# Two transformer blocks on one core: linear attention 12 and dilated attention 4 plan steps sooner, stick order turned, dilated values in 512 columns

## What is computed

```python
nx   = rmsnorm(x, attn_norm_g)
gq, gk, gv, gr, glow, dq, dk, dv = split(nx @ w_in)
o_a  = gla_mixer(gq, gk, gv, log_sigmoid(glow @ gate_w2 + gate_b) / 16)   # linear attention, 4 heads
o_a  = per_head_norm(o_a) * gla_norm_g * silu(gr)                          # gr is "gG" below
o_b  = dilated_mixer(dq, dk, dv, rel_bias)                                 # 8 heads, three patterns
h    = x + concat(o_a, o_b) @ w_out
h    = h + square(relu(rmsnorm(h) @ w_ff1)) @ w_ff2
x2   = rmsnorm(h, final_norm_g)
# second layer
q, k, v, q_hg, f_hg, i_hg, g_hg, gates = split(rmsnorm(x2) @ w_in_2)
o_sb = stick_breaking_attention(norm(q), norm(k), v)   # A = sigmoid(z) * product of (1 - sigmoid)
o_hg = hgrn2_mixer(q_hg, f_hg, i_hg, g_hg)
h    = x2 + (sigmoid(gates) * branch outputs) @ w_out_2
out  = h + (silu(hn @ w_gate) * (hn @ w_up)) @ w_down
```

## Time and profile before

| what | us |
|---|---|
| median of 3 runs | 1362.75 |
| lowest and highest of them | 1362.65, 1363.94 |
| the profiled execution, its own time | 1364.07 |
| span of the profiled execution | 1362.7 |
| PE busy in the span | 1348.6 (99%) |
| DVE busy | 873.2 (64%) |
| ACT busy | 819.9 (60%) |
| granted TensorE clock | 1.00 |

### The profile page before, as it was taken

The page is one execution under the profiler, slowest core; times in us unless marked ns, Lnnn a source line. Parts: engine busy times, 40 slices in busy tenths (PEclk is TensorE's granted clock), DMA queues, the critical chain, the costliest instruction groups (busy, mean ns, idle before and its releaser), DMA issues.

```text
span 1362.7 us, 19539 instructions
## 1 busy us (share of the span) xinstructions
PE 1348.6 (99%) x7510; PEld 1135.7 (83%) x7510; DVE 873.2 (64%) x1548; ACT 819.9 (60%) x1235; POOL 334.6 (25%) x306
## 2 busy tenths in 40 slices
PE   9999999999999999999999999999999999999999
PEld 6977956789899898887777788888888898889889
DVE  6055466577576682357787779975437785568557
ACT  6575566753544545666577767775666645754553
POOL 0211101235343251111211121211113252315214
DMA  7976643925436137876654685668888536824733
GB/s 251 238 165 144 148 117 78 231 32 196 99 98 179 33 125 191 193 169 144 149 129 111 137 217 125 137 145 182 201 214 203 110 118 194 184 47 164 188 51 109
DMA packets 57969, 202.45 MB, mean 149 GB/s; under 512 B 6450, under 2 KB 7019, under 8 KB 57748
## 3 DMA queue, kind: packets, MB, share of 16 engines
q0 software_dynamic: 25632, 93.09, 36.4%
q1 hardware_dynamic: 31380, 106.24, 23.7%
q10 hardware_dynamic: 864, 1.87, 0.4%
HBM read 199.05 MB, written 2.12 MB: 148 GB/s over the span
## 4 chain that ended last, share of the span: by engine, by line
PE 77%; DVE 11%; ACT 8%; DMA 3%; issue 2%; SPq 0%; POOL 0%; DVEq 0%; ACTq 0%
PE bank L660 18%; PE bank L667 18%; PE bank L664 18%; PE bank L698 17%; DVE eb L1730 2%; PE bank L813 1%; ACT WL L1038 1%; ACT eb L1198 1%; ACT WH L1030 1%; ACT zs L1152 1%; PE bank L885 1%; DVE eb L1725 1%; DMA WL<-in_w_in 1%; DMA WL<-in_w_gu 1%; DMA RAW<-in_w_in 1%
## 5 line engine op out<-in xcount | busy, mean ns | idle before, releaser
L660 PE MATMUL bank<-NH,WH 128*128 128x512 f32 x1152 | 459.8, 400 | 0.3 <-ACT NH L1207 0.3
L664 PE MATMUL bank<-NL,WH 128*128 128x512 f32 x1152 | 448.1, 390 | 0.6 <-DVE NL L1470 0.5
L667 PE MATMUL bank<-NH,WL 128*128 128x512 f32 x1152 | 448.1, 390 | 0.6 <-DVE WL L1465 0.4
L660 PEld LDWEIGHTS bank<-NH,WH 128*128 128x128 f32 x1152 | 216.5, 188 | 60.2 <-issue 17.8
L667 PEld LDWEIGHTS bank<-NH,WL 128*128 128x128 f32 x1152 | 216.2, 188 | 47.5 <-DVE WL L1465 0.8
L664 PEld LDWEIGHTS bank<-NL,WH 128*128 128x128 f32 x1152 | 216.8, 188 | 44.7 <-DVE NL L1470 1.6
L1030 ACT ACTIVATE WH<-RAW 128x1024 fp32r<-128x1024 f32 (+3 forms) x148 | 152.1, 1032 | 74.4 <-PE bank L667 39.0
L698 PE MATMUL bank<-AH,WH 128*128 128x256 f32 x644 | 182.5, 283 | 0.3 <-DVE AL L2115 0.3
L698 PE MATMUL bank<-AL,WH 128*128 128x256 f32 x644 | 182.2, 283 | 0.0
L698 PE MATMUL bank<-AH,WL 128*128 128x256 f32 x644 | 182.2, 283 | 0.0
L1038 ACT ACTIVATE WL<-WH 128x1024 fp32r<-128x1024 f32 (+1 forms) x146 | 153.3, 1052 | 12.2 <-DMA WH<-in_w_in 9.9
(11 more groups left out here) (375 smaller groups left out, 2115.3 us busy)
## 6 DMA issues: line engine op xcount, KB each, us to landing
WL<-in_w_in POOLq DMA_DIRECT2D x58, 512.0 KB, 7.2
RAW<-in_w_gu SPq DMA_DIRECT2D x44, 512.0 KB, 5.1
WL<-in_w_gu POOLq DMA_DIRECT2D x34, 512.0 KB, 8.0
RAW<-in_w_ff SPq DMA_DIRECT2D x32, 512.0 KB, 4.6
WH<-in_w_in POOLq DMA_DIRECT2D x32, 512.0 KB, 7.1
RAW<-in_w_in SPq DMA_DIRECT2D x28, 512.0 KB, 6.4
quarters<-in_w_ff SPq DMA_DIRECT2D x24, 512.0 KB, 4.7
WL<-in_w_ff POOLq DMA_DIRECT2D x17, 512.0 KB, 6.5
```

The source lines that it names most:

```text
L660: e.matmul(o, a[0], a[1], start=(k == 0), stop=False)
L664: e.matmul(o, b[0], b[1], start=False, stop=False)
L667: mm = e.matmul(o, c[0], c[1], start=False, stop=(k == t.kt - 1))
```

## The change

- `T_D`, the origin of the linear attention, is 12 plan steps ahead of the start of `qD`. `T_A1`, that of the dilated attention, is 4 ahead of the start of `wo0` (now called `W0`), and its period is 2.4.
- `vD` is one weight unit of 512 columns with four token tiles. Tiles 0 and 1 are interleaved block by block, then 2 and 3: two blocks of the one, two of the other, four blocks in turn, two of the one, two of the other. The copy on ACT takes 512 columns.
- In stick-breaking DVE does scan and difference for p = 0 and then for p = 1, and likewise masked copy and minimum.
- DVE's last multiplication of the `hq`, `hf` and `hg` gates moves from 9.0 (`hg`: 11.0) to 11.3, and ACT's logarithm of `hf` from 9.2 to 11.5, on the scale of `calm`.
- The `gG` sigmoids use two rows of `mixed` as scratch in place of two of the linear attention's buffers, so DVE's differences there no longer wait for gates.

```diff
-        add("vD", "w_in", 9, 11, 8, UC)
+        units.append(("vD", "w_vd", None, 8, 512, 0))
...
-                elif st == "vS" and c:
+                elif st == "vS" and c or st == "vD" and c % 2:
...
+            if st == "vD":
+                for first, second in (mine[0:2], mine[2:4]):
+                    second.v0, first.v1 = first.v0, second.v1 - 2
...
-            many = len(tiles) > 2
+            many = len(tiles) > 2 or tiles[0].st == "vD"
...
-        T_D = plan.start("qD")
-        T_A1, R1 = plan.start("wo0"), 3 * 0.71
+        T_D, W0 = plan.start("qD") - 12.0, plan.start("wo0")
+        T_A1, R1 = W0 - 4.0, 2.4
...
-            return plan.used[p - HL] + (1.3 if plan.used[p - HL] == T_A1 else 0.1)
+            return plan.used[p - HL] + (1.3 if plan.used[p - HL] == W0 else 0.1)
...
-                    yield max(t.v1 + (1.4 if t.v1 == T_A1 else 1), ready_columns[ph])
+                    yield max(t.v1 + (1.4 if t.v1 == W0 else 1), ready_columns[ph])
...
-                    n = min(t.cols, S if st == "vS" else UC)
+                    n = min(t.cols, S if st in ("vD", "vS") else UC)
...
-                    yield calm(t, 9.2)
+                    yield calm(t, 11.5)
                     act.wait_ge(("hf_f", t.i))
...
-            streams += silu_gates("gG", lambda i: mixed[:, i, :], gt_, lambda i: [("gate", "gG", i - 2)] if i >= 2 else [])
+            streams += silu_gates("gG", lambda i: mixed[:, i, :], [mixed[:, 4, :], mixed[:, 5, :]],
+                                  lambda i: [("gate", "gG", i - 2)] if i >= 2 else [("band", i)])
             streams += [gla(0), gla(1)]
-            streams += [mixed_split("mixed", k, T_A1 - 2.0 + 0.2 * k, [("gla_out", k), ("product", "block", plan.last_unit("vD"), k)])
+            streams += [mixed_split("mixed", k, W0 - 2.0 + 0.2 * k, [("gla_out", k), ("product", "block", plan.last_unit("vD"), k)])
...
-                    yield calm(t, 11.0 if st == "hg" else 9.0)
+                    yield calm(t, 9.0 if st == "gG" else 11.3)
...
-                decay(64, B64, d0, [("gla_out", 1)] if c else [("gate", "gG", 2)])
+                decay(64, B64, d0, [("gla_out", 1)] if c else [])
...
-                decay(128, B128, d1, [] if c else [("gate", "gG", 3)])
+                decay(128, B128, d1, [])
...
                             scan.then_inc(*dve.sig("stick_sum", s - 1, p))
-                        for p in range(2):
                             dve.wait_ge(("stick_sum", s - 1, p))
                             e.tensor_tensor(z[p], z[p], ee[p], ALU.subtract).then_inc(*dve.sig("stick_log", s - 1, p))
...
                             low_.then_inc(*dve.sig("stick_b", s, p))
-                        for p in range(2):
                             dve.wait_ge(("stick_b", s, p))
...
-                    yield calm(t, 9.0)
+                    yield calm(t, 11.3)
                     dve.wait_ge(("sigmoid", ("hf", t.i)), ("lb", 6))
...
+    a["w_vd"] = cut(np.ascontiguousarray(w_in[:, 2576:3088]), 8, 512)[0]
```

More of the change, by code:

```diff
@@ L2143, in vector @@
             streams += [put("qG", qG, 0.125), put("kG", kG)]
-            streams += silu_gate("gG", lambda i: mixed[:, i, :], lambda i: g_gla[:, i:i + 1], gt_, [])
+            streams += silu_gate("gG", lambda i: mixed[:, i, :], lambda i: g_gla[:, i:i + 1],
+                                 [mixed[:, 4, :], mixed[:, 5, :]], [])
             streams += [gla(0), gla(1), put("qD", qD, 0.125), put("kD", kD)]
-            streams += [mixed_split("mixed", k, T_A1 - 2.0 + 0.2 * k, []) for k in range(4)]
+            streams += [mixed_split("mixed", k, W0 - 2.0 + 0.2 * k, []) for k in range(4)]
             streams += [dilated(), to_h("wo0", "wo0", lambda k: x_in(k)[-1])]
@@ L2407, in lay_out @@
     x_t = x["x"][0].T.reshape(8, P, S).transpose(1, 0, 2).reshape(P, 8 * S)
-    a["w_in"] = cut(np.concatenate([w_in[:, 0:512], w_in[:, 768:1536], w_in[:, 1552:3088]], 1), 8, UC)
+    a["w_in"] = cut(np.concatenate([w_in[:, 0:512], w_in[:, 768:1536], w_in[:, 1552:2576]], 1), 8, UC)
+    a["w_vd"] = cut(np.ascontiguousarray(w_in[:, 2576:3088]), 8, 512)[0]
     a["w_vg"] = cut(np.concatenate([w_in[:, 512:768], w_in[:, 1536:1552]], 1), 8, UC + 16)[0]
```

## The result

The changed kernel takes 1370.22 us (median of 10 runs, 1367.45 to 1375.0) where the kernel before takes 1363.87 in the same series: a ratio of 1.0047, with an interval of 1.0037 to 1.0058, so 6.4 us slower. The prediction was 1365.0 with a range of 1356.8 to 1368.0. The direction was right, and the time lies outside the range. The profiled execution took 1370.22 us with a span of 1368.9, 6.2 more than before.

A forecast was written before the change was run, and what follows sets the result against it. PE, at full granted clock with few waits, was taken to bound the kernel. Terms -1.3 + 2.4 + 2.7 + 0.9 + 2.8 - 1.9 - 3.2 = +2.4 us on 1362.75 gave 1365.0 us, range 1356.8 to 1368.0.

The forecast's parts named there:

- the chain of the linear attention: Linear attention, c = 0: PE waits ahead of the diagonal products for work queued behind gate tile 2; +2.4 us.
- the level behind it: Linear attention, c = 0, products after the diagonal ones: lost lead and newly interposed DVE and ACT work; +2.7 us.
- c = 1: Linear attention, second pass: a weight piece and `kD`'s second copy slip ahead of its chain; +0.9 us.
- the dilated start: Dilated attention 4 steps sooner: waits at scores 1, first transposes and first value products, 4.0 for 1.2 us; +2.8 us.
- the dilated values: `vD` matmuls: 96 of 512 columns in place of 192 of 256; -1.3 us.
- its granted clock is full throughout: PE, whole kernel: the clock stays full, so edits are worth only PE work or waits removed; no clock cost counted.
- the longer period: Later dilated attention steps: the period of 2.4 gives each 0.18 us more PE work as cover; -1.9 us.
- Stick order and gates: Stick-breaking attention: later gates let DVE's chain start sooner, removing PE waits on ACT's copies; -3.2 us of 3.8.
- The turned order: Stick-breaking on DVE: dependent neighbouring instructions cost 0.5 us a step, beside a slack of about 2 us.
- The gate tiles don't hold the linear attention: Rival, faster: linear attention's 6.0 us of stalls shrink to 1 or less, giving 1359.6 or 1356.8 us; chance 0.28.
- The stick waits stay: Rival, slower: ACT's queue ahead of `vH` copies leaves only some 0.8 us gained, giving 1367.5 us; chance 0.25.

The follow-up runs named there:

- e5_gate_late: The changed kernel with ACT's Abs, Exp and Ln of the `gG` tiles due at v1 + 4 in place of v1 + 2; 1371.97 us.
- e4_fill: The changed kernel with dummy PE matmuls ahead of the linear attention's diagonal and first 256 products (c = 0) and dilated attention's first value products; 1373.71 us.
- e7_fill2: The changed kernel with dummy PE matmuls ahead of the linear attention's diagonal and first 128 products (c = 0) and dilated attention's first value products; 1368.38 us.
- e12_fill_dil: The changed kernel with linear attention back at the start of `qD`, and 6 dummy matmuls each ahead of dilated scores 1 and first value products; 1362.75 us.
- e3_both0: The changed kernel with linear attention back at the start of `qD`, dilated attention back at the start of `wo0`, and its period as before; 1360.32 us.
- e2_ta0: The changed kernel with dilated attention back at the start of `wo0` and its period back at 2.13; 1368.68 us.
- e11_period: The kernel before with the turned stick order, the later gates and dilated attention's period of 2.4 from the start of `wo0`; 1360.18 us.
- e10_gates: The kernel before with only the later `hq`, `hf`, `hg` gates and the later `hf` logarithm; 1358.26 us.
- e1_td0: The changed kernel with the linear attention back at the start of `qD`; 1362.9 us.

## Why the prediction was right or wrong

**Right: the chain of the linear attention.** 2.4 us were predicted ahead of the diagonal products and 2.44 measured, by the order on ACT that the prediction named (`e5_gate_late` takes the wait away). 2.7 us were predicted for the level behind it; at full clock 2.14 us stand ahead of the 128 products (`e4_fill`) and 0.47 at the 256 products (`e7_fill2`). The place was given (128 and 256 products), but the releaser wasn't the operand that I walked to. It was a bank, freed by a masked copy queued behind the same tile. For c = 1 0.9 was predicted: 0.47 stands ahead of its 256 products, and 0.61 ahead of an output product (L816), where the sum had no term. With the clock full in both, `e7_fill2` and `e12_fill_dil` differ, but for their dummies, by the move of the linear attention alone: 7.66 - 1.73 = 5.93 us, where the sum had 2.4 + 2.7 + 0.9 = 6.0.

**Right: the dilated start.** 4.0 us for 1.2 were predicted; 1.48 + 1.06 + 1.75 = 4.29 us are there.

**Right in half: the dilated values.** The matmuls saved 1.3 us, as counted. That merging has waits of its own stayed out of the sum; in the changed kernel the earlier dilated start hides them, alone they take it all back (`e3_both0`).

**Wrong: "its granted clock is full throughout ... so an edit is worth only what it takes from PE's work or from PE's waits."** This was read from the kernel before and carried over to a kernel to which the sum itself gave waits of 2.4, 2.7 and 1.3 us. A wait was priced at its own length. In the changed kernel the clock halves behind two of them, and the net price is 1.8 us, 9.46 against 7.66 of `e7_fill2`. The Trainium skill ("TensorE: Matmul & The Clock Gate", "Part 1: The HAM clock gate") has it that full clock is what a busy engine is given and that idling takes it away. The fall to 0.50 behind the 2.44 us agrees; the same 2.44 us in `e2_ta0` had no fall right behind them.

**Wrong: the longer period, -1.9 us.** The waits of dilated attention outside its start went from 2.0 us (3.2 less 1.06 and 0.16) to 1.6 us, so -0.4 us, and `e11_period` shows that the period by itself only moves them. The step took PE's added work as cover and forgot that DVE's and ACT's due times stretch with the same period, and the end of the attention with it. Of the two, the later end shows as the 0.9 us ahead of `wo1` in `e11_period`; the rest of the reason is read from the due times.

**Stick order and gates, -3.2 us:** -4.43 us in stretch 2. The mechanism was right for the gates, and their gain was larger than the waits that I took for the bound: 5.84 us alone, of 3.8 in the list. The bound itself was wrong. `e10_gates` runs the same PE instructions in the same order in stretch 2, so the two traces can be laid side by side: at the places of those waits PE's starts come closer by 4.5 us rather than 3.8, and 0.6 us come back at the products of the hgrn2 mixer (L885), which the prediction didn't look at. The turned order was put at 0.5 us of DVE a step, which is what the rows show, and taken to lie in a slack of 2 us. Beside the later gates it takes 5.84 - 4.66 = 1.2 us.

**The account.** In stretch 1, +5.6 predicted, +1.8 for the clock, +1.5 for the period and +0.3 for the dilated start make +9.2 of the +9.46; the rest is open. In stretch 2, 1.2 us more gain than predicted. Outside both +1.2 us, 1.0 of it behind `br0`, where the program is the same; in the other traces that part is between 0.5 us shorter and 1.5 us longer than before, so this lies within what one execution differs from another. Of the 5.2 us between 1365.0 and 1370.2, 1.1 were the low base. Neither wrong term alone explains the miss: without the clock's 1.8 us the time would be 1368.4, which is `e7_fill2`'s, without the period's 1.5 us 1368.7, both still above 1368.0; without the two it would be 1366.9.

**Rivals.** "The gate tiles don't hold the linear attention" fell with the 2.44 us. "The stick waits stay" fell too: the list after has no wait for a `vH` copy. That the clock could fall was no rival, and should have been one with a price of its own.

## What to carry to other kernels

When a sum puts a wait of a microsecond or two on an engine that has been busy throughout, give the clock a line of its own: up to what the matmuls behind the wait take twice as long, less the next wait on the same chain, which a slower PE no longer has. When a chain is moved across periodic work, count all of that work that it must let pass between two of its points; changing the order on one engine took 2.44 us from one place here and left 3.8 us at the next. And try the parts of a bundle alone: the later gates were worth 5.6 us, and the other parts gave that back and more.

## What the runs showed of the hardware

Half clock behind a wait can be nearly free: 9.17 us, most of them at half clock, against 9.03 at full clock for the same work, with 6.11 in the kernel that had no wait. What cost was the half clock with no wait left to hide it: 1.60 us behind the first value products.

Which wait is followed by a fall isn't the same each time. Waits of 2.44, 1.75 and 1.48 us were (the last in `e1_td0`), the 2.44 us of `e2_ta0`, the 2.14 of `e4_fill` and the 1.48 us of the changed kernel weren't. The runs of the changed kernel spread over 1367.5 to 1375.0 us with clocks of 0.994 to 0.999: its two at 0.999 took 1367.5 and 1367.6, those at 0.994 and 0.995 took 1374.5 and 1375.0. Those of `e10_gates`, at 1.000 throughout, spread over 1357.8 to 1359.0. Whether the falls or longer waits ahead of them make the slow ones slow, no trace shows.
